# Subtracting the low parts of the weights on GpSimd in place of VectorE beside attention, in a one-layer hybrid encoder step

## The reference

```python
def _half_ffn(x, g, w_gate, w_up, w_down):
    h = _rmsnorm(x, g)
    return x + 0.5 * ((jax.nn.silu(h @ w_gate) * (h @ w_up)) @ w_down)
...
        xp = _half_ffn(xp, g_ffn1[l], w1_gate[l], w1_up[l], w1_down[l])
        q_p, kv_p = proj(_rmsnorm(xp, g_mix[l]))
        o_p = _query_blocks(lambda qb, pb: mix(*qb, pb, *kv_p, pos_p), q_p, pos_p)
        xp = xp + o_p @ w_out[l]
        xp = _half_ffn(xp, g_ffn2[l], w2_gate[l], w2_up[l], w2_down[l])
```

## Time and profile before

| | |
|---|---|
| Median of 3 runs | 2644.37 us (2641.41 to 2650.57) |
| The profiled execution | 2648.27 us, its span 2646.5 us |
| Mean granted TensorE clock | 0.98 of full speed |
| TensorE busy | 2520.1 us (95%) |
| VectorE busy | 1447.4 us (55%) |
| ScalarE busy | 1052.0 us (40%) |
| GpSimd busy | 260.8 us (10%) |
| Subtractions `w_lo` on VectorE | 320, 386.2 us together |

### The profile page before, as it was taken

How to read it: one execution, slowest core, us unless ns; L and a number is a source line. 1 busy time by engine, 2 the same in 40 slices (tenths; PEclk the granted TensorE clock), 3 DMA queues, 4 the chain that set the end, 5 groups by cost and what they waited for, 6 DMA issues and landing times.

```text
span 2646.5 us, 36357 instructions
## 1 busy us (share of the span) xinstructions
PE 2520.1 (95%) x13547; PEld 2159.1 (82%) x13547; DVE 1447.4 (55%) x2884; ACT 1052.0 (40%) x1815; POOL 260.8 (10%) x363
## 2 busy tenths in 40 slices
PE   7999999999899999997799999999999999999997
PEld 6899999888777677776678898989888889888886
DVE  4444444444354436887544457888875544444443
ACT  3132222233233235655433347777555533222221
POOL 1000000013300000110013300000000001000000
PEclk8999999999899999998999999999999999999999
DMA  5232212323453415332342462322221131322221
GB/s 182 91 106 80 80 64 80 112 96 136 120 156 116 136 56 157 113 109 78 100 154 97 142 194 68 98 87 72 94 65 28 48 138 65 134 96 96 96 96 64
DMA packets 169004, 271.29 MB, mean 103 GB/s; under 512 B 72096, under 2 KB 104384, under 8 KB 168832
## 3 DMA queue, kind: packets, MB, share of 16 engines
q0 software_dynamic: 43200, 167.29, 18.9%
q1 hardware_dynamic: 125632, 101.69, 12.2%
HBM read 235.21 MB, written 35.29 MB: 102 GB/s over the span
## 4 chain that ended last, share of the span: by engine, by line
PE 81%; DVE 8%; issue 4%; ACT 3%; DMA 3%; SPq 1%; DVEq 0%; ACTq 0%
PE bank L1194 12%; PE bank L1196 12%; PE bank L1195 11%; PE bank L1211 6%; PE bank L1212 6%; PE bank L1213 6%; PE bank L1231 4%; PE bank L1233 4%; PE bank L1232 4%; PE bank L1321 3%; PE bank L1456 2%; DVE w_lo L1782 1%; PE bank L1290 1%; PE bank L1251 1%; PE bank L1413 1%
## 5 line engine op out<-in xcount | busy, mean ns | idle before, releaser
L1782 DVE TENSOR_TENSOR w_lo<-raw,w_hi 128x1024 fp32r<-128x1024 f32 x320 | 386.2, 1217 | 132.4 <-ACT w_hi L1496 131.6
L1194 PE MATMUL bank<-XTh_a,w_hi 128*128 128x320 f32 x1408 | 441.6, 314 | 5.3 <-DVE w_lo L1782 2.9
L1196 PE MATMUL bank<-XTh_a,w_lo 128*128 128x320 f32 x1408 | 436.7, 310 | 0.0
L1195 PE MATMUL bank<-XTl_a,w_hi 128*128 128x320 f32 x1408 | 436.6, 310 | 0.0
L1496 ACT ACTIVATE w_hi<-raw 128x1024 fp32r<-128x1024 f32 x320 | 331.1, 1046 | 176.4 <-PE bank L1233 101.1
L1211 PE MATMUL bank<-w_hi,hid_hi 128*128 128x512 f32 x792 | 323.8, 409 | 14.2 <-DVE X_b L1813 10.7
L1212 PE MATMUL bank<-w_lo,hid_hi 128*128 128x512 f32 x792 | 315.3, 398 | 0.0
L1213 PE MATMUL bank<-w_hi,hid_lo 128*128 128x512 f32 x792 | 313.2, 395 | 0.0
L1194 PE MATMUL bank<-XTh_b,w_hi 128*128 128x512 f32 x704 | 288.0, 409 | 0.0
L1813 DVE SCALAR_TENSOR_TENSOR X_a<-bank,X_a 128x512 f32<-128x512 f32 x220 | 151.2, 690 | 246.2 <-PE bank L1213 244.6
L1195 PE MATMUL bank<-XTl_b,w_hi 128*128 128x512 f32 x704 | 280.7, 399 | 0.0
(11 more groups left out here) (319 smaller groups left out, 4080.1 us busy)
## 6 DMA issues: line engine op xcount, KB each, us to landing
raw<-in_w_gate POOLq DMA_DIRECT2D x44, 1024.0 KB, 5.6
raw<-in_w_up POOLq DMA_DIRECT2D x44, 1024.0 KB, 5.7
raw<-in_w_down POOLq DMA_DIRECT2D x44, 1024.0 KB, 5.3
raw<-in_w_in POOLq DMA_DIRECT2D x16, 1024.0 KB, 5.4
s_k_in<-in_cache_diff_k SPq DMA_DIRECT2D x16, 512.0 KB, 3.8
s_v_in<-in_cache_diff_v SPq DMA_DIRECT2D x8, 1024.0 KB, 5.5
raw<-in_w_out POOLq DMA_DIRECT2D x8, 1024.0 KB, 5.4
q_rows_b<-q_scr SPq DMA_DIRECT2D x80, 64.0 KB, 2.1
```

The costliest lines, as they stand in the source:

```text
L1194: pe.matmul(out, hi[:, k], XTh[g][:, k, lo:up], start=(k == 0), stop=False)
L1195: pe.matmul(out, hi[:, k], XTl[g][:, k, lo:up], start=False, stop=False)
L1196: last = pe.matmul(out, low[:, k], XTh[g][:, k, lo:up], start=False, stop=(k == KD - 1))
L1782: dve.tensor_tensor(hilo(w_lo, u)[:, :, 0:width_of(u)], raw_part(u), hilo(w_hi, u)[:, :, 0:width_of(u)].bitcast(F32), ALU.subtract).then_i ...
```

## The change

In the two stages between `enter` and `reload` the subtraction of a unit's low part is issued by GpSimd. There it has the place in the list of items that it had on VectorE. A second semaphore, `w_ready_pool`, counts GpSimd's low parts, and `weights` waits for the one or the other, on TensorE before a unit's first product and on GpSimd before a load. Of the 320 units 103 move: 50 in the first stage and 53 in the second.

```diff
         def split_low():
             while lows:
                 n = lows.pop(0)
-                self.items.append(("split_low", n))
+                self.items.append(("pool_low" if beside else "split_low", n))
+                made = self.pool_low if beside else self.dve_low
+                made[n] = len(made)
                 if n in ended and ended[n] + RAW in loads:
                     self.items.append(("load", ended[n] + RAW))
...
         for n, item in enumerate(raw):
+            if item[0] in ("enter", "reload"):
+                beside = item[0] == "enter"
...
+        def weights(engine, u):
+            if u in plan.pool_low:
+                engine.wait_ge(w_ready_pool, plan.pool_low[u] + 1)
+            else:
+                engine.wait_ge(w_ready, plan.dve_low[u] + 1)
...
                         if c == 0:
-                            pe.wait_ge(w_ready, u + 1)
+                            weights(pe, u)
...
                     if n >= RAW:
-                        pool.wait_ge(w_ready, plan.load_end[n - RAW] + 1)
+                        for u in plan.load_units[n - RAW]:
+                            weights(pool, u)
...
+                def split(u):
+                    pool.wait_ge(w_hi_ready, u + 1)
+                    pool.tensor_tensor(hilo(w_lo, u)[:, :, 0:width_of(u)], raw_part(u), hilo(w_hi, u)[:, :, 0:width_of(u)].bitcast(F32),
+                                       ALU.subtract).then_inc(w_ready_pool, 1)
...
-                stages = {"start": start, "load": load, "square": square_rows, "mm": mm, "near_zero": near_zero, "o_square": o_square,
+                stages = {"start": start, "load": load, "pool_low": split, "square": square_rows, "mm": mm, "near_zero": near_zero, "o_square": o_square,
```

More of the change, by code:

```diff
@@ L602, in __init__ @@
         self.load_end = load_end
+        self.load_units = {}
+        for n, u in units.items():
+            self.load_units.setdefault(self.load[load_of(u)[0]], []).append(n)
         after = {}
@@ L623, in __init__ @@
         first_main = next(n for n, i in enumerate(raw) if i[0] == "gu")
-        waiting, age, lows = [], 0, []
+        waiting, age, lows, beside = [], 0, [], False
+        self.pool_low, self.dve_low = {}, {}
         for n, item in enumerate(raw):
+            if item[0] in ("enter", "reload"):
+                beside = item[0] == "enter"
             following = raw[n + 1][0] if n + 1 < len(raw) else ""
@@ L958, in build @@
         w_ready = sem("w_ready")
+        w_ready_pool = sem("w_ready_pool")
         unit_done = sem("unit_done")
```

## The result

The changed kernel took 2666.8 us (median of 4 runs, 2662.8 to 2676.6) against 2642.9 us (4 runs) for the kernel before on the same chip: a ratio of 1.009, 95% interval 1.0071 to 1.0109. That is 24 us **slower**, where 12 us faster was forecast, and outside the range. The profiled execution took 2667.8 us with a span of 2665.1 us, at the same mean granted clock, 0.98.

What follows compares the result with a forecast made beforehand. TensorE, busy nearly all the time, was taken as the bound, with 33.3 us idle where VectorE is nearly full. A 14.6 us gain less a fifth for the hold gave 12 us off the 2644.4 us median: 2632.4 us, range 2616 to 2664.

Steps and rivals of the forecast that it cites:

- the price of the hold: In the two full stretches, GpSimd's subtractions blocking VectorE's two-input operations lose 16 us, a fifth of the gain.
- The third: Share of the 49 us worst-case hold in the two full stretches taken as real: 16 us.
- The formula's upper end: Full stretches: mean wait T x T/(2 x spacing) per VectorE two-input group at 2.5 us, 49 of 84 us lost.
- The exchange: Full stretches: stopped VectorE time cancels saved time one for one, so 14.6 x 0.81 = 12 us.
- The gain: Subtractions off the chain of waits, both attention stages: 14.6 us, half of 27.2 plus 1 us elsewhere.
- My halving: Only half of the 27.2 us on the chain in the full stretches returns, the next link being close behind.
- the nothing for the clock: No gain counted for recovery of the 0.88 clock at 1210 to 1310 us, the first stage's end.
- the 5 us for one of 4.6 us: Attention norm's scale on GpSimd: a 4.6 us low part makes five of 32 late, 5 us in all.
- The first: Rival: GpSimd holds the SBUF path for its whole 2.5 us instruction; gain 6 us, 2638.4 us; chance 0.27.
- The second: Rival: the same hold with a slower low part filling VectorE's queue, at 4 us 2664 us; chance 0.17.
- The third had no wait at all: Rival: chain returns 25 of 33.7 us and the clock at 1210 to 1310 us partly recovers; 2616 us; chance 0.10.
- The fourth: Rival: the subtraction isn't on the path, so nothing changes; 2644 us; chance 0.03.

Runs made afterwards that it cites:

- e1: The change with GpSimd's 103 subtractions replaced by memsets of nearly the same length, which read nothing; result incomplete; 2613.4 us, 0.988 of the kernel before.
- e2: The change with the 103 low parts made by nobody, TensorE and loads waiting for the high part alone; result incomplete; 2612.0 us.
- e10: The change with GpSimd copying the raw weights, one SBUF input, in place of subtracting; result incomplete; 2620.3 us.
- e5: The change with each GpSimd low part cut into four back-to-back instructions of 256 columns; 2642.2 us.
- e11: The change with each GpSimd low part cut into sixteen back-to-back instructions of 64 columns; 2662.7 us.
- e13: The change with each low part in eight pieces of 128 columns, GpSimd waiting for each piece's end before the next; 2632.1 us.
- e6: The change with each GpSimd low part cut into eight back-to-back instructions of 128 columns; 2631.6 us.
- e15: Eight back-to-back pieces of 128 columns, plus the attention norm's scale issued ahead of nearby low parts and loads on GpSimd; 2627.2 us, 0.9935 of the kernel before.

## Why the prediction was wrong

**The step that failed is the price of the hold.** "The ends are 0 and 49 us; I take a third, 16 us, since the row that exists shows no wait." This was to take a fifth of the gain, 3 us; by e1 it took 53 us. Two things are wrong in it.

*The third.* The value was set by the earlier trace rows, a GpSimd operation over 8 columns, beside which VectorE's operation ran undisturbed; that is no sample of a read of 1024 columns. The right row was the earlier trace rows, in the other direction. The formula's upper end was nearer to the truth and still too low. In stretches that hold the same products, the search's (1009.3 to 1256.3 us in the change, 1009.1 to 1226.9 in e1) has 192.4 us of VectorE's busy time in the change and 154.2 in e1, 38.2 us more, where the formula said 24; the other full stretch (1610.4 to 1998.4 and 1577.5 to 1947.6 us) has 292.9 and 271.2 us, 21.7 more, where it said 26. Together 60 us, not 49 and not 16.

*The exchange.* I took stopped time and saved time to be worth the same ("14.6 x 0.81"). They aren't. The relief: 125 us of VectorE's time gave 32.8 us, 0.26 us for each (e2). The hold: 67.7 us of stretched time cost 53.4 us, 0.79 each (e1 against the change). The reason is argued and not shown: a saved microsecond lies mostly where VectorE's next operation would have waited anyway, while a stop hits an operation that is ready to go, and those with two inputs (took_a between two counts of ScalarE, ex_a before TensorE's turn, hid_lo before a product) are the ones that others wait for. TensorE's wait for ex_a L2021 fits it, 1010 to 1225 us (in all, times, longest); before it was 6.9 us, beside the memsets of e1 3.2 us:

```profile
PE bank L1319 <- DVE ex_a L2021: 10.8, 7, 6.0
```

Not all of the 53.4 us is waiting. For the same 13547 matmuls TensorE was busy for 2525.3 us in the change and for 2508.0 us in e1, 17.3 us less, at a mean granted clock of 0.980 and 0.987. In the search's stretch the two are 212.9 us at 0.92 and 204.3 us at 0.96. My sum had no term for the clock. And 0.79 isn't a constant: the shorter stops of e10 and e5 cost 0.50 and 0.64 us for each us that was stretched, in time over e1's, with intervals of about 5 us on the times.

**The gain** was also mis-sized: half of 27.2 us plus 1, 14.6 us, against 32.8 us by e2. By the first products of the units, e1 against before, 12.6 us came in the search's stretch (230.4 to 217.8 us) and 13.1 us in the second stage (from 1510 us on, 619.6 to 606.5 us), 25.7 us in all where I took 13.6; 4.0 us more came right behind the first stretch (103.7 to 99.7 us), which I had counted at nothing. As much came back as the chain had for w_lo, 33.7 us; part of it was the clock, since TensorE was busy for 12.1 us less in e1 than before. My halving, for a next link close behind, and the nothing for the clock were the error.

**What held.** GpSimd's 2.5 us (2.46). No wait of TensorE for a w_lo, and no late load: who waited for GpSimd's subtraction was its own load behind it (us, times),

```profile
  POOL raw L2291: 30.0, 51
```

and VectorE waited 0.1 us for the norm's scale. That this zero holds only for short low parts was also right, though the 5 us for one of 4.6 us was too small: with 4.6 us (e11) the waits came to 14 us, with 4.3 us (e13) to 20 us, and 3.4 us (e6) already had 6. Of the signs named, "VectorE's two-input operations grow or start late beside it" came true; "VectorE's busy time down by 125 us" did not.

**The rivals.** The first had the right mechanism, GpSimd holding for its whole instruction with 2.5 us, and still gave 2638 us, because it used the same exchange and the same small gain. The second put the break-even at T = 3.3 us; measured, 2.46 us costs 24 us net, and with one instruction a low part of 1.1 us that reads (e10) keeps 24.5 of the 32.8 us. By the square, 53.4 us x (T/2.457)^2 equals 32.8 us at a T of 1.9 us, an estimate from two lengths. The third had no wait at all, against which e1 speaks; its 2616 us is near what relief alone gives (e1, e2). The fourth, that the subtraction isn't on the path, falls by e2. The Trainium skill (SBUF — State Buffer, "SBUF: two separate sides") says that whoever starts first has the lock for the whole instruction; the timeline above agrees for a GpSimd subtraction (hid_lo ends 0.6 us behind it), and I had cited it and then priced against it. The estimate of 2.25 us from the Trainium skill (GPSIMD Engine Reference, "Elementwise — side-by-side cycle accounting") was 0.2 us short of the 2.46 us of the trace, and GpSimd's speed was not the trouble here.

## What to carry to other kernels

Before moving elementwise work from VectorE to GpSimd, count the VectorE operations with two SBUF inputs that fall in the same stretch, and those of one input from SBUF to SBUF with them, and price a stop near its full length (0.79 here, 0.50 to 0.64 for shorter stops), not at the worth of VectorE's saved time (0.26). A stop grows with the length of one instruction, so if the work must go there, cut it in pieces: eight of 0.50 us turned 24 us slower into 12 us faster. Don't cut further than that: sixteen lost all of it, back to back by new stops and with gaps by a low part of 6.5 us. Look in the trace of after for operations that got longer, since a stop shows as busy time.

## What was unexpected of the hardware

Short GpSimd instructions back to back can shut VectorE out. With 64 columns (median 0.317 us) a two-input operation stood still for up to 5.2 us and met 20 of them. With 128 columns (0.457 us) it got in after 3 at most in e6, but in e15 one stood still for 5.9 us, through 15. A gap of 78 ns between them ended it: with 64 columns 63 us of stretched time became 9. Why VectorE gets in at some ends and not at others stays open. And a copy from one SBUF tensor stops VectorE too, while a memset, which reads nothing, doesn't.
